# Mixer B of a hybrid decoder step: bias loads, cache copies and the first group merge put elsewhere in the program

## The reference

```python
for i in range(DEPTH):
    xp, xs = half_ffn(xp, i, 0, 0), half_ffn(xs, i, 0, 0)      # LayerNorm(ALPHA*x + 0.5*swiglu(x))
    if i % 2 == 0:   # layer 0, mixer A: banded attention, 16 query heads on 4 key heads, sinks
        ...
    else:            # layer 1, mixer B: qkv of 9216 columns = 3 groups x (q, k, v) x 16 heads x 64
        yp, sps = mixer_b_prompt(xp, attn_b_w_qkv[li], attn_b_w_o[li], rel_bias_table)
        ys, sss = mixer_b_sample(xs, (cache_b1_kv[li], cache_b2_kv[li], cache_b3_kv[li]), ...)
    xp, xs = post_norm(xp, yp, i, 1), post_norm(xs, ys, i, 1)
    xp, xs = half_ffn(xp, i, 1, 2), half_ffn(xs, i, 1, 2)

DILATED_GROUPS = ((128, 1), (512, 4), (2048, 16))              # (window, dilation) of a group
def combine_groups(outs, lses):                                # the merge of mixer B's groups
    w = jax.nn.softmax(jnp.stack(lses, 0), axis=0)
    return jnp.einsum('gnth,gnthd->nthd', w.astype(outs[0].dtype), jnp.stack(outs, 0))
```

## Time and profile before

| what | before |
|---|---|
| median of 3 runs | 3397.22 us (3396.34 to 3401.96) |
| the profiled execution: its own time | 3396.44 us |
| its span, first to last instruction | 3394.6 us |
| PE busy (matmuls) | 2939.0 us, 87% of the span |
| DVE / ACT / POOL busy | 1271.3 / 942.5 / 853.0 us |
| mean granted clock of PE | 0.921 of full speed |
| DMA queue q1 (SP's transfers) | 467.46 MB, 41.8% of 16 engines' span |

### The profile page before, as it was taken

The page is one execution under the profiler, slowest core; times in us unless marked ns, Lnnn a source line. Parts: engine busy times, 40 slices in busy tenths (PEclk is TensorE's granted clock), DMA queues, the critical chain, the costliest instruction groups (busy, mean ns, idle before and its releaser), DMA issues. The chain is left out here.

```text
span 3394.6 us, 53773 instructions
## 1 busy us (share of the span) xinstructions
PE 2939.0 (87%) x20802; PEld 2662.8 (78%) x20802; DVE 1271.3 (37%) x1846; ACT 942.5 (28%) x1805; POOL 853.0 (25%) x834
## 2 busy tenths in 40 slices
PE   7999988547899998999968697786964887899998
PEld 6999987417899998999967696776952222899998
DVE  2222244673422224222134123341358665422223
ACT  2222134432322214222134123131233341422212
POOL 2222122251322203222022123121226562132210
PEclk9999999758999999999989898898975888999999
DMA  6676431002566534665321331213305686366651
GB/s 231 231 241 172 159 82 35 17 15 88 177 205 205 191 127 162 207 208 191 101 87 53 99 109 55 79 52 100 104 8 178 243 290 233 101 206 205 211 170 49
DMA packets 466743, 482.09 MB, mean 142 GB/s; under 512 B 60878, under 2 KB 439871, under 8 KB 462448
## 3 DMA queue, kind: packets, MB, share of 16 engines
q1 hardware_dynamic: 456584, 467.46, 41.8%
q0 software_dynamic: 6416, 12.20, 1.3%
q10 hardware_dynamic: 3616, 0.69, 0.1%
HBM read 466.46 MB, written 199.42 MB: 196 GB/s over the span
## 5 line engine op out<-in xcount | busy, mean ns | idle before, releaser
L775 PE MATMUL bank<-sb_xh,sb_wl 128*128 128x272 f32 x4416 | 960.4, 294 | 120.0 <-DVE sb_wl L1461 92.2
L779 PE MATMUL bank<-sb_xh,sb_wh 128*128 128x272 f32 x4416 | 947.3, 291 | 0.0
L777 PE MATMUL bank<-sb_xl,sb_wh 128*128 128x272 f32 x4416 | 944.4, 291 | 0.0
L1461 DVE TENSOR_TENSOR sb_wl<-sb_raw,sb_wh 128x1024 fp32r<-128x1024 f32 (+1 forms) x340 | 452.5, 1331 | 1098.7 <-ACT sb_wh L1197 1090.1
L775 PEld LDWEIGHTS bank<-sb_xh,sb_wl 128*128 128x128 f32 x4416 | 715.3, 192 | 132.1 <-issue 69.9
L777 PEld LDWEIGHTS bank<-sb_xl,sb_wh 128*128 128x128 f32 x4416 | 715.8, 192 | 0.2
L779 PEld LDWEIGHTS bank<-sb_xh,sb_wh 128*128 128x128 f32 x4416 | 710.4, 192 | 0.0
L1197 ACT CAST sb_wh<-sb_raw 128x1024 fp32r<-128x1024 f32 (+1 forms) x340 | 376.6, 1110 | 1038.0 <-PE bank L779 934.8
L1885 POOL CAST sb_hh<-sb_h 128x544 f32 x88 | 130.2, 1480 | 735.5 <-DVE sb_h L1470 735.5
L775 PE MATMUL bank<-sb_hh,sb_wl 128*128 128x272 f32 x1408 | 311.5, 292 | 0.4 <-DVE sb_wl L1461 0.4
L779 PE MATMUL bank<-sb_hh,sb_wh 128*128 128x272 f32 x1408 | 304.2, 288 | 0.0
(11 more groups left out here) (243 smaller groups left out, 2879.2 us busy)
## 6 DMA issues: line engine op xcount, KB each, us to landing
out_state_b_s<-in_cache_b_kv SPq DMA_DIRECT2D x176, 704.0 KB, 6.3
sb_dkvb<-in_cache_b_kv SPq DMA_DIRECT2D x144, 512.0 KB, 5.6
sb_raw<-in_ffn_w_gate SPq DMA_DIRECT2D x88, 512.0 KB, 3.9
sb_raw<-in_ffn_w_up SPq DMA_DIRECT2D x88, 512.0 KB, 4.4
sb_raw<-in_ffn_w_down SPq DMA_DIRECT2D x64, 704.0 KB, 4.8
sb_raw<-in_attn_b_w_qkv SPq DMA_DIRECT2D x72, 512.0 KB, 3.9
out_state_b_s<-in_cache_b_kv SPq DMA_DIRECT2D x32, 1016.0 KB, 7.4
out_state_b_s<-in_cache_b_kv SPq DMA_DIRECT2D x4, 1984.0 KB
```

Source lines behind the costliest of these rows:

```text
L775: pe.matmul(acc(s, h), wl[slot][:, k, :], hi(k)[:, halves[h]], start=start and k == 0, stop=False)
L777: pe.matmul(acc(s, h), wh[slot][:, k, :], lo(k)[:, halves[h]], start=False, stop=False)
L779: last = pe.matmul(acc(s, h), wh[slot][:, k, :], hi(k)[:, halves[h]], start=False, stop=end)
L1461: dve.tensor_tensor(wl[j % 2][:, 0:ph.chunks, :], raw[j][:, 0:ph.chunks, :], v.bitcast(F32), ALU.subtract).then_inc(wl_rdy, 1)
```

## The change

Four things. (1) In the qkv stages `load_bias` is issued before the last turn of four unit loads (in mixer A's after the first eight units) and no longer ahead of unit 4. (2) `keep_small` is taken out of the four mixer B stages and called in each of the four down stages, after `load_first`; for layer 1's down stages this also gathers the first four `keep` copies behind the first four loads, as layer 0's have them already. (3) Round 0's merge is put into round 1: its `weights` run on DVE and ACT inside the GEMM of round 1, group 0 (at tiles 3 and 6), and its `outputs_b` between this GEMM and its attention. (4) `outputs_b` uses two pairs of banks by turns (6 and 7, 4 and 5), so that PE waits for the addition two pairs back.

```diff
@@ SP @@
-            def load_units(ph, first):
-                with sp.Fori(first, ph.units // RAW) as it:
+            def load_units(ph, first, end=None):
+                with sp.Fori(first, end or ph.units // RAW) as it:
...
                 if ph is qkv[0]:
-                    load_qkv_a(ph, range(RAW))
+                    load_qkv_a(ph, range(2 * RAW))
                     load_bias(pass_a)
-                    load_qkv_a(ph, range(RAW, ph.units))
+                    load_qkv_a(ph, range(2 * RAW, ph.units))
                 elif ph.kind == "qkv":
                     if not peeled:
                         load_first(ph)
+                    last = ph.units // RAW - 1
+                    load_units(ph, 1, last)
                     load_bias(pass_b[2 * ph.run.rnd + (ph.run.items[0][1] > 0)])
-                    n0 = 4 * ph.run.rnd + 2 * (ph.run.items[0][1] > 0)
-                    keep_small(1, n0, n0 + 2)
-                    keep_small(0, n0, n0 + 2)
+                    load_units(ph, last, last + 1)
+                elif ph.kind == "down":
+                    load_first(ph)
...
+                    for layer in range(2):
+                        keep_small(layer, 2 * ph.ffn, 2 * ph.ffn + 2)
+                    for j in range(RAW):
+                        keep(ph, 0, j)
                     load_units(ph, 1)
@@ PE @@
                 for p_ in range(4):
-                    if p_:
-                        pe.wait_ge(ot_v, PAIRS + 4 * r + p_)
+                    if p_ >= 2:
+                        pe.wait_ge(ot_v, PAIRS + 4 * r + p_ - 1)
...
-                            mm = pe.transpose(bank[6 + y][...], ...)
+                            mm = pe.transpose(bank[6 - 2 * (p_ % 2) + y][...], ...)
...
+                        if r and not y:
+                            for b in range(2):
+                                pe.wait_ge(tr_free[b], (ph.run.tr0 + ph.run.n) // 2 + 2)
+                            outputs_b(0)
+                            pe.wait_ge(ot_v, PAIRS + 4)
                         attention(pass_b[2 * r + y], ph.run)
-                        if y:
-                            outputs_b(r)
-                            if r:
-                                pe.wait_ge(sp_l, 2)
-                                decode(1)
-                            else:
-                                pe.wait_ge(ot_v, PAIRS + 4)
+                        if r and y:
+                            outputs_b(1)
+                            pe.wait_ge(sp_l, 2)
+                            decode(1)
@@ DVE, in run(ph); ACT has weights(i // 3) there @@
+                    if ph is qkv[1, 1, 0] and i in (3, 6):
+                        group_weights(0, i // 3 - 1)
...
+            def group_weights(r, y):
+                ps = pass_b[2 * r + 1]
+                dve.wait_ge(st_done, ps.u0 + ps.units)
+                dve.wait_ge(oev_done, ps.u0 + ps.units + 2)
+                weights(1 + 2 * r + y)
```

More of the change, by code:

```diff
@@ L724, in _ @@
                         load_first(ph)
+                    last = ph.units // RAW - 1
+                    load_units(ph, 1, last)
                     load_bias(pass_b[2 * ph.run.rnd + (ph.run.items[0][1] > 0)])
-                    n0 = 4 * ph.run.rnd + 2 * (ph.run.items[0][1] > 0)
-                    keep_small(1, n0, n0 + 2)
-                    keep_small(0, n0, n0 + 2)
+                    load_units(ph, last, last + 1)
+                elif ph.kind == "down":
+                    load_first(ph)
+                    if ph.l == 0 and ph.f == 0:
+                        load_norms()
+                        repeat_lines(LINE_ITS * LINE_ROWS, P - LINE_ITS * LINE_ROWS)
+                    if ph.l == 0:
+                        load_decode_constants(ph.f)
+                    for layer in range(2):
+                        keep_small(layer, 2 * ph.ffn, 2 * ph.ffn + 2)
+                    for j in range(RAW):
+                        keep(ph, 0, j)
                     load_units(ph, 1)
                 else:
[L731 to L739, removed]
-                    else:
-                        load_units(ph, peeled)
+                    load_units(ph, peeled)
                 peeled = int(ph.kind == "qkv")
@@ L996, in outputs_b @@
                 for p_ in range(4):
-                    if p_:
-                        pe.wait_ge(ot_v, PAIRS + 4 * r + p_)
+                    if p_ >= 2:
+                        pe.wait_ge(ot_v, PAIRS + 4 * r + p_ - 1)
                     for y in range(2):
                         for b in range(NBLK):
-                            mm = pe.transpose(bank[6 + y][:, b * P:(b + 1) * P], RB["o"][y][:, b, p_ * P:(p_ + 1) * P], ident[:])
+                            mm = pe.transpose(bank[6 - 2 * (p_ % 2) + y][:, b * P:(b + 1) * P], RB["o"][y][:, b, p_ * P:(p_ + 1) * P], ident[:])
                     mm.then_inc(ot_done, 1)
@@ L1302, in run @@
                         keep_tokens(act, act.copy, r, i - 1)
+                    if ph is qkv[1, 1, 0] and i in (3, 6):
+                        weights(i // 3)
                 keep_tokens(act, act.copy, r, r.n - 1)
@@ L1350, in outputs_b @@
                         act.wait_ge(ot_v, PAIRS + 4 * r + p_ - 1)
-                    act.copy(RB["st"][p_ % 2][:, 0:SEQ], bank[6][:]).then_inc(ot_a, 1)
+                    act.copy(RB["st"][p_ % 2][:, 0:SEQ], bank[6 - 2 * (p_ % 2)][:]).then_inc(ot_a, 1)
                 if r:
@@ L1434, in _ @@
                         r, y = ph.run.rnd, int(ph.run.items[0][1] > 0)
+                        if r and not y:
+                            outputs_b(0)
                         attention(pass_b[2 * r + y], ph.run)
[L1436 to L1441, removed]
+                        if r and y:
+                            weights(3)
+                            weights(4)
+                            outputs_b(1)
+                            decode(1)
                 elif ph.kind == "up":
@@ L1654, in outputs_b @@
                     v = RB["at"][:, p_, :].rearrange("p (u c) -> p u c", c=4)
-                    y = bank[7][:].rearrange("p (c u) -> p u c", c=4)
+                    y = bank[7 - 2 * (p_ % 2)][:].rearrange("p (c u) -> p u c", c=4)
                     x = RB["st"][p_ % 2][:, 0:SEQ].rearrange("p (u c) -> p u c", c=4)
@@ L1836, in _ @@
                         r, y = ph.run.rnd, int(ph.run.items[0][1] > 0)
+                        if r and not y:
+                            outputs_b(0)
                         attention(pass_b[2 * r + y], ph.run)
[L1838 to L1846, removed]
+                        if r and y:
+                            group_weights(1, 0)
+                            group_weights(1, 1)
+                            outputs_b(1)
+                            decode(1)
                 elif ph.kind == "up":
```

1 line of the change is left out of this document (removed).

## The result

| what | before | after |
|---|---|---|
| median of 6 runs each, in turn on one chip | 3397.19 us (3396.34 to 3402.11) | 3414.80 us (3411.11 to 3415.61) |
| ratio to before, with 95% interval | | 1.0045 [1.0033, 1.0057] |
| the profiled execution: own time, span | 3396.44, 3394.6 us | 3415.03, 3413.2 us |
| PE busy, mean granted clock | 2939.0 us, 0.921 | 2937.0 us, 0.921 |

A forecast was written before the change was run, and what follows sets the result against it. PE, busy 87% of the span, was taken as the bound, so edits count by its idle time and clock. Gains of 117 us against 126 us lost in the down stages gave +9 us on 3396.4: 3406 us, range 3384 to 3428.

The forecast's parts named there:

- The core: Mixer B and down stages: small copies hold two DMA engines 47 to 49 us; weight loads behind wait; down waits 95-145 us.
- Rival 1: Down stages: the copies cost nothing there, since four long units give enough cover; 3279 us, chance 0.06.
- Rival 2: Down stages: the `keep` copies of the burst don't delay unit 4; loss 102 us, time 3382 us, chance 0.12.
- Rival 3: Down stages: a second stall in each, from unit 5's load handed over late; some 6 us a stage, 3430 us, chance 0.12.
- Rival 4: Mixer: gives less, as PE waits elsewhere in these stages, above all round 1, group 0; some 20 us, 3426 us, chance 0.08.
- The down stages: Four down stages: PE waits at unit 4 behind the moved copies, 118 us, plus 2 us half clock each: 126 us lost.
- Moving the bias costs nothing: Qkv stages: the later bias load still has 4 units, 26 us, of cover; in mixer A nothing to gain: 0.
- Mixer B's three holes: Mixer B, unit 4: PE's three waits of 67.7 us go, with 6 us of half clock behind them.
- The boundary: Between rounds 0 and 1: round 0's merge leaves it, giving back 44.2 us including 1.4 us of half clock.
- `weights` in the GEMM: Round 1, group 0's GEMM: each holds DVE 4.84 us, costing PE 0.5 us each, 1 us; bounds 0 and 8.
- `outputs_b(0)`: On PE before round 1's first attention: costs 4.2 us net of the former wait for staged queries; bounds 2 and 8.
- `outputs_b(1)`: Round 1's merge: three PE waits of 1.40 us go with two pairs of banks, 4.2 us gained.

The follow-up runs named there:

- e1: Changed kernel with every sequence's rows in the small copies cut into 16 pieces, the pieces made the outermost dimension: 3286.06 us, ratio 0.9674.
- e3: Changed kernel with all eight sequences' small copies at once in layer 1's first down stage, outermost dimension 8: 3304.76 us, ratio 0.9727.
- e2: Changed kernel without the small copies: 3280.97 us, ratio 0.9652.
- e9: Changed kernel with 16-way small copies only in layer 1's down stages, mixer A's bias still after eight units: 3278.36 us; same with bias after four: 3273.41 us.
- e4: Kernel before with only the small copies moved to the down stages (layer 1's first four `keep` copies gathered with it): 3440.68 us, ratio 1.0120.
- e5: Kernel before with only the small copies cut 16 ways, copies and bias loads at their old places: 3313.77 us, ratio 0.9751.
- e6: Changed kernel with 16-way small copies and round 0's merge back between the rounds, two pairs of banks kept: 3306.14 us, ratio 0.9727.
- e7: Changed kernel with 16-way small copies and `outputs_b` on one pair of banks again: 3306.40 us, ratio 0.9731.

## Why the prediction was right, and where it was not

**The core held.** A pair of copies with outermost dimension 2 runs on two engines, and what SP issues behind it waits. e1 changes the number of engines alone (16); e3 makes it 8 and gathers the copies in one stage; the holes follow in both. This agrees with the rule that the prediction cites from the Trainium skill (page "DMA: Bandwidth & Descriptors", section "Why a DMA increments its semaphore by 16 and not by 1"), by which these copies use 2, 8 and 16 engines: the shares were 0.12, 0.48 and 1.03. Rival 1 (free copies, 3279 us) falls by the four holes, though its time is nearly e2's 3281, the kernel without them. Rival 2 falls by its loss, 132.8 and not 102 us. That unit 4 waits for the `keep` copies too is read from the sizes alone (62.4 us from the copies to PE, where the prediction's terms without the 6.1 us of the `keep` copies give 54); no run leaves them out. Rival 3 falls: after each hole PE ran on without another. Its premise held, though: SP stayed 48.78 us (from 322.81) in issuing the `keep` copy behind unit 4's load and handed over unit 5's at 371.87 us, which was still in time. Rival 4 falls: mixer B gave more, not less.

**The down stages: 126 us forecast, 132.8 measured.** Waits 124.1 for 118 (44.65, 38.54, 20.42 and 20.53 for 42.6, 36.8, 19.3 and 19.3), half clock 3.3 to 5.2 us after each hole. What the four stages take beyond the waits, 8.7 us, is the term that the prediction had at 8. The undersized term is the time from the copies to PE's unit 4: 62.4, 61.9, 63.1 and 63.2 us for 60.3 and 61.8.

**"Moving the bias costs nothing ... In mixer A's stage PE has no wait that it could remove: 0"** is the step that failed: mixer A takes 6.7 us more in the profile after (in the seven profiles with the late bias its GEMM stage takes 0.6 to 8.8 us more than in the five without, see e9). I asked what the move could remove and whether the bias still had cover, not whom its transfers would meet. They met POOL's small stores, which DVE and ACT wait for. With this step at 6.7 and the down stages at 132.8 the forecast would have been 3419 us; mixer B gave some of it back.

**Mixer B's three holes: 73.7 forecast, 72.7 measured** (17.9 + 26.5 + 28.3). But the prediction credited "copies or a waiting bias load": e4 and e5 show that it was the narrow copies alone, as the bias is still ahead of unit 4 in both.

**The boundary: 44.2 forecast, 44.2 measured, and yet not what moving the merge is worth.** e4 has the merge in its old place and the copies gone: its wait is 12.7 us shorter (29.87 - 17.18). e6 has nothing of SP's there: 12.76 us. So of the 44 us some 17 were the exchange of POOL slowed by SP's transfers, another 6 are the one pair of banks with its half clock (from the first transpose to the next unit 13.4 us, 7.2 in e6), and a quiet boundary with two pairs costs 19 (e6 against e1), of which some 15 are gained by moving the merge. Two parts of the exchange are slowed by different transfers. POOL's own store makes it wait 1.46 us in e6, 5.88 with the bias alone (e4), 7.22 with bias and narrow copies (before) and 8.73 with bias and wide copies (e5). Its fetches land after at most 13.3 us beside the narrow copies, but after 2.3 to 2.4 us in e4, e5 and e6. As in mixer A, a small transfer of POOL's is late beside SP's large ones. The prediction took the 19.65 us of the earlier trace rows as they stood and did not ask what made them.

**The merge's parts.** `weights` in the GEMM 1 forecast, 0.6 measured; `outputs_b(0)` 4.2 forecast, 2.7 measured: two waits of 0.5 to 0.9 us and one of 1.40, and full clock. `outputs_b(1)` with the decoding part behind it 4.2 forecast, 9.3 measured. e7 puts the pairs of banks at 5.8 us of it, of which 1.7 are clock; the rest, 3.5 us, was not isolated, and it is about what two profiles of one kernel differ by there (3.0 us). All gains together came to 122.9 us for 117, above the stated bound of 121. (The two terms with bounds give 106 to 120, not the 108 to 121 that the prediction states.)

Sum: +6.8 (down stages), +6.7 (mixer A), -5.9 (mixer B) and +2.0 (elsewhere) against +9 make the +18.6 us. The forecast was a small difference of two sums near 120 us, and it came out at half of what was measured. That the kernel got slower, and not faster, hung on 9 us; that the miss stayed at 9 us is in part luck, since the errors have both signs.

## What to carry to other kernels

Before weighing where a bulk copy should stand, look at how many DMA engines it uses: a share of 0.12 of 16 with loads outstanding says two. A copy on two engines delays what is behind it in the queue by its whole length (here 47 to 49 us); moving it moves the hole to the stage that it is moved to, cutting it 16 ways removes it (129 us in the changed kernel, 84 in the one before, for one line). And when a transfer is moved, ask which small transfers on another queue it will fly beside, and which engine waits for them.

## What was not expected of the hardware

- POOL's stores of 16 KB mostly land in 1.7 us with the early bias, and in up to 14.1 us beside SP's four bias loads of 512 KB; a wait of POOL for its own store of maxima and sums is 1.46 us alone and 7.22 us beside bias and copies. Whether the DMA engines' order or the memory makes it so was not tried.
- After a hole PE stayed at half clock for 3.3 to 5.2 us in the down stages, though it was busy throughout. In e7 PE ran at half clock from 2428.9 us through the whole of round 1's merge with its holes of 1.4 us, and in round 0's it fell to half clock between such holes; in e1, with one hole of 0.2 us, it had full clock for the last two pairs. Two pairs of banks were worth more than the waits they take away.
